# Depthwise convolution of 31 taps: one accumulator in PSUM for all taps instead of one in PSUM and one in SBUF

## The reference, cut to what matters

```python
z = u @ w_in
a, b, gate = jnp.split(z, 3, axis=-1)
c = a * jax.nn.sigmoid(b)
full = jnp.concatenate([buf.astype(c.dtype), c], axis=1)
y = lax.conv_general_dilated(full, conv_w[:, None, :], window_strides=(1,), padding='VALID',
    dimension_numbers=('NWC', 'WIO', 'NWC'), feature_group_count=D_CONV)
y = y + conv_b
y = jax.nn.silu(layer_norm(y, ln_g, ln_b))
out = (y * jax.nn.silu(gate)) @ w_out
```

## Time and profile before

| | |
|---|---|
| time, median of 3 runs | 3381.7 us (3375.78 to 3386.1) |
| span of the profiled execution, first to last instruction | 3378.6 us |
| PE busy | 3197.5 us, 95% |
| DVE busy | 1511.2 us, 45% |
| POOL busy | 1551.1 us, 46% |
| ACT busy | 854.5 us, 25% |
| mean granted clock of PE | 0.974 |
| end of the convolution stage (last L1316 ends) | 894.8 us into the span |

### The profile page before, as it was taken

The page is one execution under the profiler, slowest core; times in us unless marked ns, Lnnn a source line. Parts: engine busy times, 40 slices in busy tenths (PEclk is TensorE's granted clock), DMA queues, the critical chain, the costliest instruction groups (busy, mean ns, idle before and its releaser), DMA issues.

```text
span 3378.6 us, 50475 instructions
## 1 busy us (share of the span) xinstructions
PE 3197.5 (95%) x19117; PEld 3077.4 (91%) x19117; DVE 1511.2 (45%) x1745; ACT 854.5 (25%) x1708; POOL 1551.1 (46%) x1153
## 2 busy tenths in 40 slices
PE   7999999999899999999778999999999999999995
PEld 6999999999899999999668998999899899899995
DVE  6999999999711131000560433244323343500043
ACT  5121121121222132212321322222222222332232
POOL 2777877878543324333353223332233223144475
PEclk9999999999899999999899999999999999899998
DMA  4122122122132252212453112111111211333386
GB/s 158 45 64 58 46 69 58 46 69 58 57 100 87 93 171 78 73 63 70 170 190 94 36 37 63 41 37 44 47 47 41 53 38 46 118 114 87 97 295 217
DMA packets 171677, 284.87 MB, mean 84 GB/s; under 512 B 62008, under 2 KB 72504, under 8 KB 171576
## 3 DMA queue, kind: packets, MB, share of 16 engines
q1 hardware_dynamic: 127328, 222.48, 22.2%
q10 hardware_dynamic: 41912, 52.32, 4.2%
q0 software_dynamic: 2352, 8.88, 0.7%
HBM read 218.44 MB, written 67.15 MB: 85 GB/s over the span
## 4 chain that ended last, share of the span: by engine, by line
PE 57%; POOL 17%; issue 12%; DVE 6%; DMA 4%; ACT 2%; SPq 1%; POOLq 0%; ACTq 0%; DVEq 0%
PE z_odd L512 9%; PE z_odd L513 8%; PE z_odd L515 8%; PE z_even L512 8%; PE z_even L513 7%; PE z_even L515 7%; POOL w_lo L1013 6%; POOL work L1094 4%; PE aux L609 3%; POOL work L1086 3%; PE z_even L627 2%; DMA work<-conv_scratch 1%; PE z_even L629 1%; POOL work L1122 1%; DMA work<-out_scratch 1%
## 5 line engine op out<-in xcount | busy, mean ns | idle before, releaser
L1013 POOL TENSOR_TENSOR w_lo<-w_raw,w_hi 128x512 fp32r<-128x512 f32 x528 | 746.7, 1423 | 1452.1 <-ACT w_hi L730 1451.6
L512 PE MATMUL z_even<-u_hi,w_hi 128*128 128x364 f32 (+1 forms) x2784 | 925.1, 332 | 80.7 <-POOL u_lo L1174 33.8
L512 PE MATMUL z_odd<-u_hi,w_hi 128*128 128x364 f32 (+1 forms) x2784 | 939.0, 337 | 58.9 <-POOL w_lo L1013 58.9
L513 PE MATMUL z_odd<-u_lo,w_hi 128*128 128x364 f32 (+1 forms) x2784 | 922.5, 331 | 0.0
L513 PE MATMUL z_even<-u_lo,w_hi 128*128 128x364 f32 (+1 forms) x2784 | 921.0, 331 | 0.0
L730 ACT ACTIVATE w_hi<-w_raw 128x512 fp32r<-128x512 f32 x528 | 331.4, 630 | 1730.5 <-PE z_even L515 810.3
L515 PE MATMUL z_odd<-u_hi,w_lo 128*128 128x364 f32 (+1 forms) x2784 | 636.5, 330 | 0.0
L515 PE MATMUL z_even<-u_hi,w_lo 128*128 128x364 f32 (+1 forms) x2784 | 635.3, 329 | 0.0
L512 PEld LDWEIGHTS z_even<-u_hi,w_hi 128*128 128x128 f32 x2784 | 529.8, 190 | 99.6 <-issue 30.7
L512 PEld LDWEIGHTS z_odd<-u_hi,w_hi 128*128 128x128 f32 x2784 | 531.7, 191 | 97.3 <-POOL w_lo L1013 55.1
L513 PEld LDWEIGHTS z_odd<-u_lo,w_hi 128*128 128x128 f32 x2784 | 532.1, 191 | 0.1
(11 more groups left out here) (148 smaller groups left out, 2405.1 us busy)
## 6 DMA issues: line engine op xcount, KB each, us to landing
w_raw<-in_w SPq DMA_DIRECT2D x528, 256.0 KB, 2.7
work<-in_x SPq DMA_DIRECT2D x32, 544.0 KB, 5.7
work<-branch_scratch SPq DMA_DIRECT2D x31, 544.0 KB, 5.5
conv_scratch<-work ACTq DMA_DIRECT2D x16, 544.0 KB, 2.7
work<-conv_scratch SPq DMA_DIRECT2D x16, 544.0 KB, 3.7
resid_scratch<-work ACTq DMA_DIRECT2D x16, 544.0 KB, 6.2
branch_scratch<-work ACTq DMA_DIRECT2D x16, 512.0 KB, 2.6
branch_scratch<-work POOLq DMA_DIRECT2D x15, 544.0 KB, 3.0
```

Of the source, the lines that this page charges most:

```text
L512: pe.matmul(o, w_hi[:, q, at:at + P], chunk(u_hi[:, k, :], c), start=(i == 0), stop=False)
L513: pe.matmul(o, w_hi[:, q, at:at + P], chunk(u_lo[:, k, :], c), start=False, stop=False)
L1013: pool.tensor_tensor(w_lo[:, q, :], w_raw[:, q, :], w_hi[:, q, :].bitcast(F32), ALU.subtract).then_inc(w_lo_ready, 1)
```

## The change

All 31 taps of the prompt go to the accumulator in PSUM. `odd_taps` and the last addition are gone. Each tap now waits for the tap just before it. The last tap itself signals `conv_ready`. On DVE the piece for the samples is written first, and the signal `cp_head` is given when 728 positions of `cp` stand; ACT makes tap 0 in two pieces, 728 positions behind `cp_head` and 296 behind `z_read`.

```diff
-        (r_a, sig, y_st, y_sq, acc_y, acc_y2, cp, cs_flat, ys, prod, odd_taps) = places(
-            T, T, T, T, T, T, TP + 32, SB * SEG, TS, 4 * SS * CW, TP)
+        (r_a, sig, y_st, y_sq, acc_y, acc_y2, cp, cs_flat, ys, prod) = places(
+            T, T, T, T, T, T, TP + 32, SB * SEG, TS, 4 * SS * CW)
...
+                n = CHUNKS[0][1] + CHUNKS[1][1]
+                tap0 = dict(scale=cols[:, bass.ds(C_CW + j * CW, 1)], bias=cols[:, bass.ds(C_CB + j, 1)])
+                act.wait_ge(cp_head, j + 1)
+                act.activation(aux1[:, 0:n], cp[:, 0:n], ACT.Identity, **tap0)
                 act.wait_ge(z_read, 2 * j + 2)
-                act.activation(aux1, cp[:, 0:TP], ACT.Identity, scale=cols[:, bass.ds(C_CW + j * CW, 1)],
-                               bias=cols[:, bass.ds(C_CB + j, 1)]).then_inc(tap0_ready, 1)
+                act.sem_inc(act_passed, 1)
+                act.activation(aux1[:, n:TP], cp[:, n:TP], ACT.Identity, **tap0).then_inc(tap0_ready, 1)
...
+                dve.tensor_tensor(cs[:, :, HIST:SEG], z_odd[:, 2, left:left + TS].rearrange("p (b t) -> p b t", b=SB),
+                                  sig[:, TP:T].rearrange("p (b t) -> p b t", b=SB), ALU.mult)
                 dve.tensor_tensor(cp[:, HIST:HIST + n0], z_odd[:, 0, 0:n0], chunk(sig, 0), ALU.mult)
...
+                dve.tensor_tensor(cp[:, HIST + n0:HIST + n0 + n1], z_odd[:, 1, 0:n1], chunk(sig, 1), ALU.mult
+                                  ).then_inc(cp_head, 1)
                 dve.tensor_tensor(cp[:, HIST + n0 + n1:HIST + TP], z_odd[:, 2, 0:left],
...
+                                  sig[:, n0 + n1:TP], ALU.mult).then_inc(z_read, 1)
 
                 dve.wait_ge(z_read, 2 * j + 2)
-                dve.tensor_scalar(odd_taps, cp[:, 1:1 + TP], cols[:, bass.ds(C_CW + j * CW + 1, 1)], None,
-                                  ALU.mult).then_inc(tap, 1)
                 dve.wait_ge(tap0_ready, j + 1)
-                for i in range(2, CW):
-                    if i > 2:
-                        dve.wait_ge(tap, (CW - 1) * j + i - 2)
-                    acc = odd_taps if i % 2 else aux1
-                    dve.scalar_tensor_tensor(out=acc, in0=cp[:, i:i + TP],
-                                             scalar=cols[:, bass.ds(C_CW + j * CW + i, 1)], in1=acc,
-                                             op0=ALU.mult, op1=ALU.add).then_inc(tap, 1)
+                for i in range(1, CW):
+                    if i > 1:
+                        dve.wait_ge(tap, (CW - 2) * j + i - 1)
+                    dve.scalar_tensor_tensor(out=aux1, in0=cp[:, i:i + TP],
+                                             scalar=cols[:, bass.ds(C_CW + j * CW + i, 1)], in1=aux1,
+                                             op0=ALU.mult, op1=ALU.add
+                                             ).then_inc(tap if i < CW - 1 else conv_ready, 1)
                     if i == CW // 2 and nxt:
                         read_z(2 * j + 2, z_even, sig, r_a)
-                dve.wait_ge(tap, (CW - 1) * j + CW - 1)
-                dve.tensor_tensor(aux1, aux1, odd_taps, ALU.add).then_inc(conv_ready, 1)
```

More of the change, by code:

```diff
@@ L216, in trunk_kernel @@
         pe_passed = sem("pe_passed")
+        act_passed = sem("act_passed")
         dve_passed = sem("dve_passed")
@@ L223, in trunk_kernel @@
         hist_in = sem("hist_in")
+        cp_head = sem("cp_head")
         tap0_ready = sem("tap0_ready")
@@ L1293, in glu @@
                 n0, n1 = CHUNKS[0][1], CHUNKS[1][1]
+                left = TP - n0 - n1
+                dve.tensor_tensor(cs[:, :, HIST:SEG], z_odd[:, 2, left:left + TS].rearrange("p (b t) -> p b t", b=SB),
+                                  sig[:, TP:T].rearrange("p (b t) -> p b t", b=SB), ALU.mult)
                 dve.tensor_tensor(cp[:, HIST:HIST + n0], z_odd[:, 0, 0:n0], chunk(sig, 0), ALU.mult)
-                dve.tensor_tensor(cp[:, HIST + n0:HIST + n0 + n1], z_odd[:, 1, 0:n1], chunk(sig, 1), ALU.mult)
@@ L1296, in glu @@
-                left = TP - n0 - n1
+                dve.tensor_tensor(cp[:, HIST + n0:HIST + n0 + n1], z_odd[:, 1, 0:n1], chunk(sig, 1), ALU.mult
+                                  ).then_inc(cp_head, 1)
                 dve.tensor_tensor(cp[:, HIST + n0 + n1:HIST + TP], z_odd[:, 2, 0:left],
-                                  sig[:, n0 + n1:TP], ALU.mult)
-                dve.tensor_tensor(cs[:, :, HIST:SEG], z_odd[:, 2, left:left + TS].rearrange("p (b t) -> p b t", b=SB),
-                                  sig[:, TP:T].rearrange("p (b t) -> p b t", b=SB), ALU.mult).then_inc(z_read, 1)
+                                  sig[:, n0 + n1:TP], ALU.mult).then_inc(z_read, 1)
```

## The result

The changed kernel takes 3353.35 us (median of 4 runs, 3346.77 to 3354.78), the kernel before 3381.76 in the same comparison: ratio 0.9912, 95% interval 0.9900 to 0.9924. It is 28 us faster where 38 were forecast.

A forecast was written before the change was run, and what follows sets the result against it. The prediction took DVE's loop in the convolution stage as the bound: 5.3 + 28 × 1.42 + (1.195 + 1.33) + 1.28 = 48.9 us a step against 51.1. The stage gains 38 us: 3381.7 − 38 = 3344 us, range 3332 to 3356.

The forecast's parts named there:

- DVE's loop bounds the stage, by its SBUF taps: Convolution stage: DVE's loop sets the 51.1 us step; SBUF taps wait for POOL's running instruction, 1875 ns against 1277 on PSUM.
- The wait for the tap before, taken from the first tap's pair: DVE taps in the loop: address instruction, then tap, starts 0.14 us after what it waits for, so 1.42 us a tap.
- Tap 0 in two pieces: ACT's tap 0 in each step: costs 0.2 us more than now; the early signal helps nothing while DVE is the bound.
- End to first tap: Step boundary on DVE: from one convolution's end to the next step's first tap, forecast 5.3 us.
- The sum: Convolution stage: DVE's terms give 48.9 us a step against 51.1, ending at 856.7 us, not 894.76; gain 38 us.
- its own sum for the kernel before: DVE's step in the kernel before, its terms added in the prediction: 50.8 us against 51.1 measured.
- Nothing is given back: Behind step 15: the path through ACT, POOL and PE counts from the convolution's end, so the 38 us stay.
- PE next late by `w_lo`: PE in the convolution steps: leads until POOL's quarter `w_lo` stops it, waiting 1 to 2 us a step.
- PE-bound rival: Convolution stage: the tap wait is hidden, 1.32 us a tap, PE bounds at 47.6 us a step; 3325 us, chance 0.14.
- The rule against moving the accumulator: Skill rule to copy PSUM to SBUF first; by it only waits would remain, some 80 us lost; the prediction rejected it.

The follow-up runs named there:

- run 6: Kernel before with one accumulator for all taps, but in SBUF, tap 0 in one piece: 3593.4 us, ratio 1.0620.
- run 8: Kernel before with GpSimd's product of sigmoid and norm factor taken over 64 of 1088 columns: 3344.86 us, ratio 0.9888.
- run 9: Changed kernel with GpSimd's product of sigmoid and norm factor taken over 64 of 1088 columns: 3352.62 us.
- Run 3: Kernel before, both accumulators kept, each tap made to wait for the tap directly before it: 3438.07 us, ratio 1.0168.
- run 4: Changed kernel with the step's 31 tap weights first copied to a fixed place, so no address instruction precedes a tap: 3323.44 us, ratio 0.9835.
- run 1: Kernel before with only the one accumulator in PSUM; tap 0 in one piece, gated input in its old order: 3345.2 us, ratio 0.990.
- run 7: Kernel before with most of GpSimd's tree of additions in the sample convolution left out: 3377.29 us, ratio 0.9982.

## Why the prediction was right, and where it was off

*DVE's loop bounds the stage, by its SBUF taps.* Right. Runs 6, 8 and 9 show that these taps and GpSimd exclude each other, and that PSUM taps are free of it. The POOL instruction at 525.41 us that the prediction calls an addition is the product of sigmoid and norm factor (L1069), the one that run 8 shortens; the reading of its times is right. The Trainium skill, GPSIMD Engine Reference, Key points, names contention of GpSimd with VectorE instructions that have two SBUF inputs. The runs agree and add its form and size: a held tap ends 1.08 us after GpSimd's instruction.

*The wait for the tap before, taken from the first tap's pair.* Right in its mechanism. The wait is 1.433 − 1.289 = 0.144 us, forecast 0.14. Run 3 shows it without the change, run 4 removes the address instruction and leaves 0.035. The tap itself was taken at 1.276, as it lasts when it follows its neighbour without a pause; it lasts 1.289 when it starts on an idle engine, which makes 28 × 0.013 = 0.4 us a step. This is the larger part of what the sum had too small.

*Tap 0 in two pieces.* Right in sign, 0.28 us against 0.2 (run 1). End to first tap is 5.46, forecast 5.3. Half of the difference is the pieces, 0.95 and 0.58 long; the other half is that the first tap starts 0.23 us behind ACT's end (529.94 − 529.71) and not 0.14 as before, in the whole-piece run too (527.66 − 527.43). With L1303 gone, the first tap waits for `z_read` and for tap 0, and the trace has one waiting instruction of DVE more ahead of it.

*The sum.* The end of the convolution was forecast at 856.7 and came at 866.0, 28.8 us before the old 894.8 and not 38. The 9.3 us are: 2.3 at the end of step 1 (178.6, forecast 176.3), 13 × 0.5 from steps of 49.4 and not 48.9, and 0.4 in step 15. Of the 2.3, 1.4 stand already at the first tap of step 0 (86.6 against 85.2); it comes between 85.3 and 87.2 us in the eleven traces, those of both accumulators included, so that this part is the spread between executions and not a fault of the sum. The term of the prediction that was mis-sized is the length of the loop: 48.9 us, measured 49.4, 1% of itself. Since only 2.2 us a step were to be won, that 1% is a quarter of the gain. The prediction had a sign of it: its own sum for the kernel before gave 50.8 us, 0.3 less than measured, yet the 2.2 are the difference of the measured 51.1 and a sum made in the same way. Sum against sum it would have been 1.9, with 1.7 measured. The lesson is in the difference of two near numbers, not in the mechanism.

*Nothing is given back.* Right as far as the end of the stage goes: PE's start behind it moved by 28.8, and the median by 28.4. The span of the profiled execution shrank by 25.5; the 3 us between lie in the last 500 us, at waits for DMA, and the medians don't confirm them.

*PE next late by `w_lo`.* Right in place: from 501 us on it waits there once a step, eight times, 1.3 to 1.7 us each.

*PE-bound rival.* It needed 1.32 us a tap, and run 4 shows that it holds then, with 3323 us where 3325 was worked out. The Trainium skill, VectorE: DVE Perf Modes, The DRAIN you can't avoid, reports that a semaphore after each of eight chained copies cost nothing extra. Here a wait for the tap before costs 0.13 us a tap even at its cheapest (1.325 against 1.19) and 0.24 with the address instruction, so the runs disagree with it for this operation.

*The rule against moving the accumulator.* For elementwise work on a matmul's output, the Trainium skill, VectorE: DVE Perf Modes, Rules for kernel authors, gives the choice of accepting the rate from PSUM or copying to SBUF first if many operations follow. For this chain beside a busy GpSimd the second choice is the wrong one: with all taps in PSUM the kernel is 1% faster than before (run 1), with all in SBUF 6% slower (run 6).

## What to carry to other kernels

In these traces a float32 VectorE instruction with two inputs in SBUF waits for the instruction that GpSimd is running (1.27 us become up to 3.64), and holds GpSimd's next one in turn (2.63 us become 6.53 for four). If GpSimd is busy beside a chain that matters, try one operand in PSUM, or make GpSimd's longest instruction shorter, even if GpSimd seems to have time. When every instruction waits for the one before, look at which instruction carries the wait: here, with a loop-dependent address ahead, the address was computed after the wait (0.11 us a tap), and a copy of the step's constants to a fixed place took it away. Work out what engine comes next before expecting more: here 1.8 us a step lay between VectorE's loop and TensorE's.

## What was not expected of the hardware

A tap lasts 1289 ns when the engine had idled before it, be it for 0.035 us (run 4) or 0.144 (runs 1 and 3), and 1276 when it starts before its neighbour has ended. And the interplay with GpSimd is not in proportion to GpSimd's work: in run 7 the two trees of a step took 4.6 us in place of 9.8 and the whole kernel gained 6 us; in run 8 one instruction of 2.5 us a step was cut short and it gained 37.
